# A fused two-block kernel: first FFN tiles on an unnormalized split, moved reload waits, and retention by halves of the sequence

## What is computed

```python
def reference(x, ...):               # x: (1, 1024 tokens, 1024)
    # first block
    mix = concat(forgetting_attention, conformer_conv, multiscale_pool)  # from rms_norm(x) @ w_in
    x = x + mix @ w_out
    h2 = rms_norm(x, norm2_g)
    up = causal_depthwise_conv(h2 @ w_up, ffn_dw_w)       # width 3, 2 x 2816 channels
    gate, val = split(up); x = x + (silu(gate) * val) @ w_down
    # second block, layer 0: retention, 8 heads
    proj = rmsnorm(x) @ w_in_a
    o = retention(rope(q), rope(k), v)                    # group-normed per head
    x = x + rmsnorm((o * silu(gate)) @ w_out_a)
    # layer 1: differential attention, 8 heads, w_out_b
    return x + rmsnorm((o * silu(gate)) @ w_out_b)
```

## Time and profile before

| what | value |
|---|---|
| median of 3 runs | 2874.92 us (2872.38 to 2877.82) |
| the profiled execution | 2874.93 us |
| its span, first to last instruction | 2873.3 us |
| TensorE busy | 2754.4 us, 96% |
| VectorE busy | 1602.8 us, 56% |
| ScalarE busy | 685.3 us, 24% |
| mean granted clock of TensorE | 0.988 |

### The profile page before, as it was taken

One profiled execution on the slowest core, in us unless ns is written; L12 is line 12 of the kernel. 1 busy time (PEld: TensorE's weight loads), 2 busy tenths in 40 slices (PEclk: granted clock), 3 DMA queues, 4 the chain that ended last, 5 costly groups with the idle time before them and its releaser, 6 DMA issues.

```text
span 2873.3 us, 35595 instructions
## 1 busy us (share of the span) xinstructions
PE 2754.4 (96%) x13508; PEld 2204.9 (77%) x13524; DVE 1602.8 (56%) x1975; ACT 685.3 (24%) x1246; POOL 325.1 (11%) x310
## 2 busy tenths in 40 slices
PE   8989988999999999999999999999999999999996
PEld 6757756778888888877888888888776888888774
DVE  7765553545555445564554554454466666666654
ACT  2233341211111111121011011011033434444431
POOL 0699800000000000021000000000000000000000
PEclk9999999999999999999999999999999999999998
DMA  4211212234343433424222222222233222222131
GB/s 169 88 59 59 73 45 103 88 117 163 134 165 138 146 146 117 162 101 161 73 73 88 77 81 76 88 73 73 88 132 132 74 73 75 86 76 74 55 128 63
DMA packets 48634, 286.61 MB, mean 100 GB/s; under 512 B 6592, under 2 KB 6720, under 8 KB 18624
## 3 DMA queue, kind: packets, MB, share of 16 engines
q1 hardware_dynamic: 21776, 118.50, 11.8%
q0 software_dynamic: 14544, 105.91, 10.8%
q10 hardware_dynamic: 12256, 61.39, 5.6%
HBM read 248.03 MB, written 29.36 MB: 97 GB/s over the span
## 4 chain that ended last, share of the span: by engine, by line
PE 85%; DVE 9%; ACT 3%; issue 2%; DMA 1%; DVEq 0%; ACTq 0%; SPq 0%
PE PB L241 12%; PE PB L243 12%; PE PB L242 12%; PE OBB L241 9%; PE OBB L243 9%; PE OBB L242 9%; PE TBB L784 3%; PE TBB L241 2%; PE TBB L242 2%; PE TBB L243 2%; PE PB L833 2%; PE OBB L898 2%; PE PB L839 1%; PE OBB L893 1%; DVE on L2079 1%
## 5 line engine op out<-in xcount | busy, mean ns | idle before, releaser
L241 PE MATMUL PB<-HH,WH 128*128 128x512 f32 x1488 | 586.1, 394 | 25.7 <-DVE A L555 9.2
L243 PE MATMUL PB<-HH,WL 128*128 128x512 f32 x1488 | 581.8, 391 | 0.0
L242 PE MATMUL PB<-HL,WH 128*128 128x512 f32 x1488 | 581.7, 391 | 0.0
L241 PE MATMUL OBB<-HH,WH 128*128 128x512 f32 x1024 | 417.2, 407 | 7.6 <-DVE WL L257 5.2
L243 PE MATMUL OBB<-HH,WL 128*128 128x512 f32 x1024 | 402.1, 393 | 0.0
L242 PE MATMUL OBB<-HL,WH 128*128 128x512 f32 x1024 | 401.7, 392 | 0.0
L241 PEld LDWEIGHTS PB<-HH,WH 128*128 128x128 f32 x1488 | 281.1, 189 | 91.6 <-issue 28.5
L242 PEld LDWEIGHTS PB<-HL,WH 128*128 128x128 f32 x1488 | 281.0, 189 | 60.1 <-issue 1.9
L243 PEld LDWEIGHTS PB<-HH,WL 128*128 128x128 f32 x1488 | 280.8, 189 | 58.9
L257 DVE TENSOR_TENSOR WL<-RAW,WH 128x2048 fp32r<-128x2048 f32 x101 | 234.6, 2323 | 65.3 <-DMA WH<-units 31.8
L2319 POOL DMA_DIRECT2D WH<-units x85 | 45.6, 536 | 1886.0 <-PE PB L241 1132.0
(11 more groups left out here) (350 smaller groups left out, 3981.8 us busy)
## 6 DMA issues: line engine op xcount, KB each, us to landing
RAW<-units SPq DMA_DIRECT2D x85, 1024.0 KB, 4.7
WH<-units POOLq DMA_DIRECT2D x85, 1024.0 KB, 5.1
gs<-units ACTq DMA_DIRECT2D x16, 1024.0 KB, 4.8
gu<-gs ACTq DMA_DIRECT2D x16, 1024.0 KB, 3.9
RAW<-gu SPq DMA_DIRECT2D x16, 1024.0 KB, 4.9
WH<-gu POOLq DMA_DIRECT2D x16, 1024.0 KB, 5.3
tmpd<-xr SPq DMA_DIRECT2D x112, 64.0 KB, 2.0
A<-xT SPq DMA_DIRECT2D x4, 1024.0 KB, 9.5
```

The lines of the kernel that those rows point to most:

```text
L241: first = pe.e.matmul(out, wh, xh, start=start, stop=False)
L242: pe.e.matmul(out, wh, xl, start=False, stop=False)
L243: return pe.e.matmul(out, wl, xh, start=False, stop=stop), first
```

## The change

In the output projections tiles go round four banks instead of two. In `w_out`, VectorE splits the next unit before it waits for the reload, and that wait moves to tile 2; tiles 6 and 7 run as one unit with the input tile in the outer loop, marking each input tile when it is done with (`k{k}`). ScalarE and VectorE then split A times the norm's gain, without the root, into HH and HL. The first FFN unit works on that; the total of the squares stands inside it; VectorE multiplies its two results by the root in their banks (`scaled_g`, `scaled_v`) between normalized tiles 4 and 5. The second unit of `ffn_first` takes the normalized tiles and writes TBB and OBB. The filler and the three-engine wait ahead of the FFN loop on TensorE are gone; TensorE waits there for `cv0_0`, and before a down step for the last `y` of the iteration before. In retention the second value's transposes use another bank, the normed output is turned, gated and split by halves h of the sequence, and the first three output tiles are done in two passes of one half each. TBB and OBB change places in the output tiles.

```diff
+        act.e.wait_ge(pe_done, at_mark(act, "pe", "total"))
+        roots(act, PB[0], rbn)
     else:
         act.e.preload_act_table_set(LN_EXP)
-    act.e.wait_ge(pe_done, at_mark(act, "pe", "total"))
-    roots(act, PB[0], rbn)
+        act.e.wait_ge(pe_done, done_in("pe", "ffn_first", "total"))
+        roots(act, TBB, rbn)
...
+        if squares == "summed":
+            act.e.wait_ge(pe_done, done_in("pe", "ffn_first", "v0_0" if k == KT - 1 else f"k{k}"))
         act.e.activation(HH[:, k, :], tmn[:, k % 2, :], ACT.Copy).then_inc(act_done, act.mark(f"hi{k}"))
...
+        if squares == "summed" and k == 4:
+            for b, x in enumerate("gv"):
+                dve.e.wait_ge(pe_done, done_in("pe", "ffn_first", f"{x}0_0"))
+                dve.e.tensor_tensor(PB[b][:, :], PB[b][:, :], rbn[:, :], ALU.mult).then_inc(
+                    dve_done, dve.mark(f"scaled_{x}"))
...
+    pe.e.wait_ge(dve_done, done_in("dve", before, "y4"))
...
+OUT_BANKS = [PB[0], PB[1], TBB, OBB] * 2
+
 def out_pe(pe, ph, u0, after, order):
     pe.start(ph, after)
     dense_unit(pe, PB, u0 % 2, HH, HL, ((None, "d0"), (None, "d1")), order, None, True)
     for m in range(2, KT):
         if m % 2 == 0:
             slot = unit(pe, u0 + m // 2)
-        if m >= 2:
-            pe.e.wait_ge(dve_done, at_mark(pe, "dve", f"y{m - 2}"))
-        dense(pe, PB[m % 2], slot, m % 2, HH, HL, f"d{m}")
+        if m == 6 and ph == "w_out":
+            pe.e.wait_ge(dve_done, at_mark(pe, "dve", "y3"))
+            dense_unit(pe, OUT_BANKS[6:], slot, HH, HL, ((None, "d6"), (None, "d7")), range(KT), None, False,
+                       lambda k: f"k{k}")
+            break
+        if m >= 4:
+            pe.e.wait_ge(dve_done, at_mark(pe, "dve", f"y{m - 4}"))
+        dense(pe, OUT_BANKS[m], slot, m % 2, HH, HL, f"d{m}")
...
         square_act(act, k, lambda k: f"y{k}")
+        if add and k == 5:
+            for j in range(6):
+                raw_high(act, j)
+    if add:
+        for j in (6, 7):
+            raw_high(act, j)
+
+def raw_high(act, k):
+
+    act.e.wait_ge(dve_done, at_mark(act, "dve", f"y{k}"))
+    act.e.wait_ge(pe_done, at_mark(act, "pe", "d7" if k == KT - 1 else f"k{k}"))
+    act.e.activation(HH[:, k, :], A[:, k, :], ACT.Copy, scale=p_("norm2", k, 1)).then_inc(
+        act_done, act.mark(f"hi{k}"))
 def out_dve(dve, ph, u0, add, nth=0):
     dve.start(ph)
-    if add:
-        dve.e.wait_ge(reloaded, 16 * nth)
     low_part(dve, u0 + 1)
     for m in range(KT):
+        if add and m == 2:
+            dve.e.wait_ge(reloaded, 16 * nth)
         dve.e.wait_ge(pe_done, at_mark(dve, "pe", f"d{m}"))
         if add or m < 2:
-            ins = dve.e.tensor_tensor(A[:, m, :], A[:, m, :], PB[m % 2][:, :], ALU.add)
+            ins = dve.e.tensor_tensor(A[:, m, :], A[:, m, :], OUT_BANKS[m][:, :], ALU.add)
         else:
-            ins = dve.e.tensor_copy(A[:, m, :], PB[m % 2][:, :])
+            ins = dve.e.tensor_copy(A[:, m, :], OUT_BANKS[m][:, :])
         ins.then_inc(dve_done, dve.mark(f"y{m}"))
-        if m % 2 == 0 and m and u0 + m // 2 + 1 < NU:
-            low_part(dve, u0 + m // 2 + 1)
-        if m >= 2:
+        if m in ((2, 4, 5) if add else (2, 4)):
+            low_part(dve, u0 + (m + 1) // 2 + 1)
+        if add and m == 5:
             sum_dve(dve, m - 1)
+            sum_dve(dve, m)
+            for k in range(6):
+                gained_low(dve, k, "norm2")
+        elif m >= 2 and not (add and m >= 6):
+            sum_dve(dve, m - 1)
+    if add:
+        sum_dve(dve, KT - 2)
     sum_dve(dve, KT - 1)
+    if add:
+        for k in (6, 7):
+            gained_low(dve, k, "norm2")
...
+def up_bank(b, j, i):
+
+    return FF_OUT[b] if i is None and j else PB[b]
...
+def first_total(pe):
+
+    pe.e.wait_ge(dve_done, done_in("dve", "w_out", f"acc{KT - 1}"))
+    halves(pe, TBB, ones[:, :], sqn[:, 0, :], "total")
+
 def ffn_pe(pe, ph, steps, u0, n=None):
-    pe.start(ph, "norm2" if ph == "ffn_first" else None)
+    pe.start(ph, {"ffn_first": "w_out", "ffn_loop": "ffn_first", "ffn_last": None}[ph])
+    if ph == "ffn_loop":
+        pe.tiles_of = None
+        pe.e.wait_ge(dve_done, done_in("dve", "ffn_first", "cv0_0"))
...
+                    if i is None:
+                        if j:
+                            pe.tiles_of = "norm2"
+                        dense_unit(pe, (PB, FF_OUT)[j], slot, HH, HL,
+                                   ((None, f"g{s}_{j}"), (None, f"v{s}_{j}")), range(KT),
+                                   None if j else lambda k: first_total(pe) if k == 1 else None, False,
+                                   None if j else lambda k: f"k{k}")
                         continue
...
                 elif i is not None:
-                    pe.e.wait_ge(dve_done, at_last(pe, "dve", "lo2_1", i))
+                    pe.e.wait_ge(dve_done, at_last(pe, "dve", f"y3_{KT - 1}", i))
...
-        if steps[0][0] == "up":
-            warm(pe, TBB, 5)
...
+                if i is None and j == 0 and s == 0 and ph == "ffn_first":
+                    act.e.wait_ge(dve_done, done_in("dve", "norm2", "scaled_v"))
...
-                if j == 0 and i is None:
-                    low_part(dve, u0 + 1)
...
-                    if b == 0 and not (j == 0 and i is None):
+                    if i is None and j == 0 and b:
+                        low_part(dve, u0 + 2)
+                    elif i is not None and b == 0:
                         low_part(dve, u0 + offs[s] + j + 1, i, 6)
...
-RET_OUT = [PB[0], PB[1]] + [TBB, OBB] * 3
+RET_OUT = [PB[0], PB[1]] + [OBB, TBB] * 3
+VALUE_BANKS = [[TB[0], TB[1]], [OB[1], TB[0]]]
...
+    def out_half(m, h, slot, name):
+        cols = slice(h * HALF, (h + 1) * HALF)
+        for f in range(2):
+            c = f * 1024 + m * P
+            mm, first = mm3(pe, RET_OUT[m][:, cols], WH[slot][:, c:c + P], WL[slot][:, c:c + P],
+                            yH[:, f, cols], yL[:, f, cols], f == 0, f == 1)
+            if pe.fresh:
+                first.then_inc(unit_begun, 1)
+                pe.fresh = False
+        if name:
+            mm.then_inc(pe_done, pe.mark(name))
...
         for f in range(2):
+            pe.e.wait_ge(dve_done, at_mark(pe, "dve", f"v{f}", i))
             for g in range(2):
-
-                pe.e.wait_ge(act_done, at_mark(pe, "act", f"vt{f - 1}_{g}" if f else f"kt{g}", i))
-                pe.e.wait_ge(dve_done, at_mark(pe, "dve", f"v{f}", i))
-                transposes(pe, TB[g], lambda b: vR[:, f, b * P:(b + 1) * P],
+                if (f, g) != (1, 0):
+                    pe.e.wait_ge(act_done, at_mark(pe, "act", "vt0_0" if f else f"kt{g}", i))
+                transposes(pe, VALUE_BANKS[f][g], lambda b: vR[:, f, b * P:(b + 1) * P],
...
-        for f in range(2):
-            for g in range(2):
-
-                pe.e.wait_ge(dve_done, at_mark(pe, "dve", f"yt0_{g}" if f else f"on{4 * g + 3}", i))
-                transposes(pe, TB[g], lambda b: on[:, b, f * P:(f + 1) * P],
-                           range(4 * g, 4 * g + 4), f"ot{f}_{g}")
-            if f == 0:
+        for h in range(2):
+            if h:
                 gate(1, 1, slot, i)
+            pe.e.wait_ge(dve_done, at_mark(pe, "dve", f"on{4 * h + 3}", i))
+            for f in range(2):
+                if h:
+                    pe.e.wait_ge(dve_done, at_mark(pe, "dve", f"yt{f}_0", i))
+                transposes(pe, TB[f], lambda b: on[:, b, f * P:(f + 1) * P],
+                           range(4 * h, 4 * h + 4), f"ot{f}_{h}")
         slot = unit(pe, u0 + 3, i, 4)
-
-        pe.e.wait_ge(dve_done, at_mark(pe, "dve", "lo0", i))
-        for m in range(2):
-            dense(pe, RET_OUT[m], slot, m, yH, yL, None, nk=1, toff=P, stop=False)
-        pe.e.wait_ge(dve_done, at_mark(pe, "dve", "lo1", i))
-        for m in range(2):
-            dense(pe, RET_OUT[m], slot, m, yH, yL, f"d{m}", nk=1, koff=1, woff=1024, toff=P, start=False)
-        for m in range(2, KT):
-            if m == 2:
-                pe.e.wait_ge(dve_done, at_mark(pe, "dve", "yt1_1", i))
-            elif m > 3:
+        for h in range(2):
+            pe.e.wait_ge(dve_done, at_mark(pe, "dve", ("lo_0", "lo1_1")[h], i))
+            for m in range(3):
+                out_half(m, h, slot, f"d{m}" if h else None)
+        for m in range(3, KT):
+            if m > 3:
                 pe.e.wait_ge(dve_done, at_mark(pe, "dve", f"y{m - 2}", i))
             dense(pe, RET_OUT[m], slot, m, yH, yL, f"d{m}", nk=2, kstride=1024, toff=P)
...
+        gate(1, 0, i)
+        act.e.wait_ge(dve_done, at_mark(act, "dve", "yt1_0", i))
+        e.activation(yH[:, :, 0:HALF], yt[:, :, 0:HALF], ACT.Copy).then_inc(act_done, act.mark("hi_0"))
+        gate(1, 1, i)
         for f in range(2):
-            gate(1, f, i)
             act.e.wait_ge(dve_done, at_mark(act, "dve", f"yt{f}_1", i))
-            e.activation(yH[:, f, :], yt[:, f, :], ACT.Copy).then_inc(act_done, act.mark(f"hi{f}"))
```

(32 more changed lines are left out.)

## The result

The changed kernel takes 2825.32 us in the median of 4 runs (2821.74 to 2826.61), the kernel before 2874.78 beside it. The ratio is 0.9825, with a 95% interval of 0.9808 to 0.9842. The forecast was 2827.5, with a range of 2819.5 to 2841. The profiled execution, at 2826.61 the slowest of the four, has a span of 2824.9 us, 48.4 less than before; the medians differ by 49.5.

The account below looks back on a forecast made before the run. TensorE, busy 96% of 2873.3 us, was taken as the bound, with only pauses, filler and half-clock matmuls to win. Gains 33.4 + 13.2 + 0.8 = 47.4 left 2825.9, with 1.6 around it 2827.5 us; range 2819.5 to 2841.

Parts of the forecast that it names:

- Part 1: Start of the first output projection: TensorE no longer pauses for y0 behind the reload of A; gain 10.7 us.
- Part 2: Before the first FFN unit: no filler, root or normalized tile to wait for, 12.2 less 1.7 for the total; gain 10.5.
- Part 3: Second FFN unit's wait for its bank goes, 2.9 us; border before the FFN loop goes, 9.2; parts 1 to 3 together 33.4.
- The fetch of instructions at a loop's entry: FFN loop's entry: an unknown wait, between nothing and 2.4 us, taken as 0 as it can overlap another wait.
- Part 4: Retention, 8 heads: three pauses go, a new wait before output tile 4 costs 0.8; gain 1.65 us per head, 13.2 in all.
- Rival C: Retention: the new wait before output tile 4 is hidden, 6.4 us less, 2821.1; chance 0.10.
- (a): Retention, second value's transposes: a free bank removes a wait of 0.33 + 0.17, 0.05 stays; 0.45 us per head.
- (b): Retention, first-half transposes of the normed output need only on3, so a wait of 0.58 + 0.17 goes; 0.75 us per head.
- Part 5: Second output projection: TensorE's wait for y0, 0.7 + 0.17, goes; gain 0.8 us.
- rival F: Whole kernel slower than before: with pauses gone the chip grants less clock; 2920 us at 0.90; chance 0.02.
- The warning that equal pauses may end at either level: Clock behind pauses of about 2.7 us: 2.4 or 1.2 GHz, some 2 us at each of two left in retention.
- The reading that short pauses stand unpunished: Clock: short pauses bring no half clock behind them; pauses of 0.97 us were followed by full speed.

Follow-up runs that it names:

- Experiment 3: The changed kernel, but VectorE waits for the reload of A ahead of its split of unit 13, as before; four banks stay: 2833.23 us, ratio 0.9859.
- Experiment 4: The changed kernel, but TensorE waits for the end of the first FFN stage on all three engines before the loop: 2836.70 us, ratio 0.9878.
- experiment 5: The changed kernel, with the total of the squares behind k = 5 instead of k = 1 of the first FFN unit: 2836.35 us, ratio 0.9863.
- experiment 6: The changed kernel, with the split of the next unit behind y2 instead of y1 in retention: 2816.51 us, ratio 0.9797.
- experiment 7: The changed kernel, with retention's first split of each head moved ahead of the border: 2816.03 us, ratio 0.9793.
- experiment 8: The changed kernel with the edits of experiment 6 and experiment 7 together: 2812.60 us; again 2809.97, beside the changed kernel's 2822.20.
- experiment 1: The kernel before with the retention part of the change alone: 2859.70 us against 2872.75, ratio 0.9954.

## Why the forecast was right, step by step

| term | forecast | measured in the profiled executions |
|---|---|---|
| attention's end to the FFN loop (parts 1 to 3) | 33.4 | 33.6 |
| FFN loop to retention's first v | 0 | 0.0 |
| retention, first v to the last total's norm (part 4) | 13.2 | 14.0 |
| the rest (part 5) | 0.8 | 1.4 |
| start to attention's end | 0 | -0.6 |
| sum | 47.4 | 48.4 |

**Part 1.** Right in place and size. Experiment 3 shows what I had not separated: the place of the reload wait carries most of the part. DMA issues of the changed kernel between 430 and 620:

```profile
A<-xT ACTq DMA_DIRECT2D x1, 3072.0 KB, 15.1
```

The reload, issued at 456.88, took 15.1 us instead of 10.4, beside the two transfers of unit 14, which are now issued at 459.42 and 463.51. In experiment 3, where these two are again issued only behind the reload, it took 10.1. The 15 us that I had allowed as the bad case are thus the rule. It landed near 472.0, and `y2` began at 473.63; 1.6 us more and the sum would have been late, though with the next split wanted only at 484 it would have cost nothing yet.

**Part 2.** Right by the trace; no run takes the unnormalized split out by itself. The total costs 1.32 to the next start and 0.40 more in the one behind, 1.72, as taken. The wait for unit 16's transfer (5.16) was covered.

**Part 3.** Right, to 0.2: TensorE entered at 573.2 where 573.4 stood. Experiment 4 confirms the price of the border, and experiment 5 that VectorE's chain has no slack behind tile 4. The fetch of instructions at a loop's entry, bounded at 0 to 2.4, shows nothing here: TensorE's one wait there ends with VectorE's split.

**Part 4.** Right in mechanism: three pauses gone, and the forecast new one there, 0.80 for 0.8. The last low ended 2.98 behind the start of the output part, as forecast (3.0). The gain was a little larger than its term: 1.78 a head (periods of mostly 105.70 and 103.92) for 1.65. From the starts, (a) brought 0.51 for 0.45, (b) 0.80 for 0.75, and the output part 0.47 for 0.45. Rival C (wait hidden) is out by the row of eight waits; experiment 6 shows its cause, VectorE's order of y1, split, y2.

**Part 5.** 1.4 for 0.8. The wait for `y0` is gone; what the other 0.6 are was not traced, and neither were the 0.6 by which this execution came later to the end of attention. The latter made the gain smaller, not larger.

**Clock.** No stretch of the changed kernel's FFN loop fell under 1.00, so rival F is out. The warning that equal pauses may end at either level held. The reading that short pauses stand unpunished held for those of 0.5 us in retention (0.51 for the first matmul behind one), not for those of 2.71 and 2.48 at its loop's ends, behind which the profiled execution ran at half clock (0.79 and 0.70). I did not apply the warning in the expectations of experiments 7 and 8, and missed that of experiment 8 by it.

## What to carry to other kernels

When one engine is busy 96% of the time, list its pauses, ask for each which step of the other engine's program order ends it, and move that step ahead of waits that it doesn't need; here one wait moved past one split was worth 8 to 11 us. A stage border that waits for all engines can be replaced by the one mark that the next stage's first write needs. Price the new order's own waits by the same arithmetic: the 0.8 us before tile 4 could be seen before the run, and removing it took one line.

## What I had not expected of the hardware

The clock behind one and the same pause of 2.7 us differed between executions of the same code (first matmul 0.79 or 0.49, mean 0.83 or 1.00 over the stretch behind). So one profile can't price such a dip, and a difference of a few us between single executions means little: seven executions of the kernel before, in one set, lie between 2871.95 and 2879.52. And a load of 3 MB took 10.1 to 10.4 us in the three profiles in which no other transfer was issued before it landed (before, experiments 1 and 3), and 15.1 to 16.1 in the nine in which two transfers of 1 MB were issued 2.5 and 6.6 us behind it.
